# First attention of a two-block transformer: probability tiles turned by diagonal matrices of the shares

## What is computed

```python
def softmax_attend(q, k, v, scale):
    s = jnp.einsum('bqhd,bkhd->bhqk', q, k).astype(jnp.float32) * scale
    p = jax.nn.softmax(s, axis=-1).astype(v.dtype)
    return jnp.einsum('bhqk,bkhd->bqhd', p, v)
...
def window_attend(q, k, v, k_ctx, v_ctx, sink):
    ...
    sink_col = jnp.broadcast_to(sink.reshape(SWA_KV_HEADS, SWA_GROUP, 1, 1).astype(jnp.float32),
                                s_ctx.shape[:-1] + (1,))
```

## Time and profile before

| | us |
|---|---|
| median of 3 runs | 1627.12 (1625.2 to 1627.42) |
| the profiled execution, its own time | 1628.66 |
| its span in the trace | 1626.7 |
| first attention, unit 2's scores to the output projection (109.8 to 237.5 in the span) | 127.7 |
| PE busy in the whole span | 1554.0 |

### The profile page before, as it was taken

One profiled execution on the slowest core, in us unless ns is written; L12 is line 12 of the kernel. 1 busy time (PEld: TensorE's weight loads), 2 busy tenths in 40 slices (PEclk: granted clock), 3 DMA queues, 4 the chain that ended last, 5 costly groups with the idle time before them and its releaser, 6 DMA issues.

```text
span 1626.7 us, 26737 instructions
## 1 busy us (share of the span) xinstructions
PE 1554.0 (96%) x11163; PEld 1203.2 (74%) x11163; DVE 819.1 (50%) x1434; ACT 730.7 (45%) x1122; POOL 0.9 (0%) x5
## 2 busy tenths in 40 slices
PE   8999989999999999999989999999999889999887
PEld 5645667777787778789968999997998778544443
DVE  2536664643333444453486665655686775322123
ACT  3544552633312332362464654535545553554443
POOL 0000000000000000000000000000000000000000
PEclk9999999999999999999999999999999999999999
DMA  9412633344433442433203346453443337899995
GB/s 390 162 39 79 208 109 114 115 156 185 147 122 149 161 157 79 161 110 130 79 1 119 117 150 225 165 165 116 165 139 121 105 102 287 360 420 420 421 420 211
DMA packets 43130, 287.87 MB, mean 177 GB/s; under 512 B 4848, under 2 KB 6000, under 8 KB 12160
## 3 DMA queue, kind: packets, MB, share of 16 engines
q1 hardware_dynamic: 42832, 285.99, 47.1%
q10 hardware_dynamic: 144, 0.06, 0.0%
q0 software_dynamic: 32, 0.07, 0.0%
HBM read 285.05 MB, written 1.05 MB: 176 GB/s over the span
## 4 chain that ended last, share of the span: by engine, by line
PE 80%; DVE 8%; ACT 5%; DMA 5%; issue 2%; SPq 0%; DVEq 0%; ACTq 0%
PE ps L542 16%; PE ps L544 15%; PE ps L543 15%; PE ps L2969 7%; DMA deep<-wts 4%; DVE WL L527 2%; PE ps L593 2%; PE ps L1572 1%; PE ps L1543 1%; PE ps L1474 1%; PE ps L711 1%; PE ps L2830 1%; PE ps L1651 1%; PE ps L1649 1%; PE ps L1650 1%
## 5 line engine op out<-in xcount | busy, mean ns | idle before, releaser
L542 PE MATMUL ps<-HH,WH 128*128 128x256 f32 (+3 forms) x1424 | 467.8, 329 | 14.3 <-DVE WL L527 6.3
L543 PE MATMUL ps<-HL,WH 128*128 128x256 f32 (+3 forms) x1424 | 456.8, 321 | 0.0
L544 PE MATMUL ps<-HH,WL 128*128 128x256 f32 (+3 forms) x1424 | 456.6, 321 | 0.0
L527 DVE TENSOR_TENSOR WL<-ring,WH 128x2048 fp32r<-128x2048 f32 (+2 forms) x134 | 281.6, 2104 | 143.3 <-ACT WH L517 143.3
L542 PEld LDWEIGHTS ps<-HH,WH 128*128 128x128 f32 x1424 | 269.6, 189 | 59.2 <-issue 26.3
L517 ACT ACTIVATE WH<-ring 128x2048 fp32r<-128x2048 f32 (+2 forms) x134 | 236.0, 1763 | 152.1 <-PE ps L544 76.1
L544 PEld LDWEIGHTS ps<-HH,WL 128*128 128x128 f32 x1424 | 269.7, 189 | 20.3
L543 PEld LDWEIGHTS ps<-HL,WH 128*128 128x128 f32 x1424 | 269.9, 190 | 18.2
L2969 PE MATMUL ps<-deep,arena 128*32 128x512 f32 (+1 forms) x872 | 115.3, 593 | 15.5 <-ACT deep L2955 6.8
L542 PE MATMUL ps<-parts,WH 128*128 128x512 f32 (+1 forms) x352 | 120.0, 341 | 0.0
L543 PE MATMUL ps<-parts,WH 128*128 128x512 f32 (+1 forms) x352 | 118.5, 337 | 0.0
(11 more groups left out here) (394 smaller groups left out, 2127.2 us busy)
## 6 DMA issues: line engine op xcount, KB each, us to landing
ring<-wts SPq DMA_DIRECT2D x138, 1024.0 KB, 5.0
deep<-wts SPq DMA_DIRECT2D x92, 1024.0 KB, 18.4
ring<-wts SPq DMA_DIRECT2D x32, 704.0 KB, 4.1
arena<-wts SPq DMA_DIRECT2D x8, 1024.0 KB, 15.4
ring<-wts SPq DMA_DIRECT2D x4, 672.0 KB, 13.7
X<-xin SPq DMA_DIRECT2D x4, 512.0 KB, 16.4
ahead<-wts SPq DMA_DIRECT2D x2, 1024.0 KB, 8.1
deep<-wts SPq DMA_DIRECT2D x4, 512.0 KB, 20.7
```

The source lines that it names most:

```text
L527: e.tensor_tensor(lo, raw(i), hi.bitcast(F32), ALU.subtract).then_inc(*up("low", i))
L542: e.matmul(o, w[0][:, cols], x[0], start=k == 0, stop=False)
L543: e.matmul(o, w[0][:, cols], x[1], start=False, stop=False)
L544: return e.matmul(o, w[1][:, cols], x[0], start=False, stop=k == nk - 1)
```

## The change

Each probability tile is now turned by a real product with a diagonal matrix that holds the shares, instead of by a transpose with the identity; so the turned probabilities are already divided. `share_of` names the diagonal matrices: 64 in all, two for a lat unit and four for a context unit, in three buffers of two matrices each that are used in turn. DVE builds them in `dve_share` (the identity times a share column, a 128x128 TENSOR_SCALAR each), now one step earlier (unit i-1 instead of i-2) and behind the maxima of unit i instead of ahead of them. `pe_values` no longer spreads shares. The copy to `OT` and its multiplication are gone: ACT writes the rounded part straight from PSUM, one step earlier, behind its copy of the turned probabilities; DVE takes the remainder straight from PSUM, where it multiplied before. The bank of an output tile is now freed by that remainder (`o_low`) instead of `o_unit`.

```diff
-        OT = area(256)
+        DG = [area(256)] + [deep[:, a:a + 256] for a in (9 * SLOT + 4096, 9 * SLOT + 16 * NT + 4096)]
...
-                if 0 <= i - 4:
-                    act_values_high(e, i - 4)
...
                 if 0 <= i - 3 < len(UNITS):
-                    act_values(e, i - 3)
+                    act_values_high(e, i - 3)
...
-                if 0 <= i - 2 < len(UNITS):
-                    dve_share(e, i - 2)
                 if i < len(UNITS):
                     dve_scores(e, i)
+                if 0 <= i - 1 < len(UNITS):
+                    dve_share(e, i - 1)
                 if 0 <= i - 4:
-                    dve_values(e, i - 4)
+                    dve_values_low(e, i - 4)
...
-                if 0 <= i - 4:
-                    dve_values_low(e, i - 4)
...
             e.reciprocal(columns(rv, j), c).then_inc(*up("weighed.share", j))
+            e.wait_ge(*at("weighed.share", j))
+            if j >= 2:
+                e.wait_ge(*at("turned_p", j - 2, 1))
+            for s in range(2):
+                for q in range(query_tiles(j)):
+                    t = e.tensor_scalar(share_of(j, s, q), ident, column(rv, j, s, q), None, ALU.mult)
+            t.then_inc(*up("weighed", j))
+        def share_of(j, s, q):
+            n = sum(2 * query_tiles(x) for x in range(j)) + s * query_tiles(j) + q
+            return DG[n // 2 % 3][:, 128 * (n % 2):128 * (n % 2) + 128]
...
                 e.wait_ge(*at("exp", j, s))
+                e.wait_ge(*at("weighed", j))
                 for x in range(4):
-                    c = 128 * x if lat else 256 * (x % 2) + 128 * (x // 2)
-                    t = e.transpose(ps[:, b, 128 * x:128 * x + 128], PA3[j % 3][s][:, c:c + 128], ident)
+                    c, q = (128 * x, 0) if lat else (256 * (x % 2) + 128 * (x // 2), x % 2)
+                    t = e.matmul(ps[:, b, 128 * x:128 * x + 128], PA3[j % 3][s][:, c:c + 128],
+                                 share_of(j, s, q), start=True, stop=True)
...
-            e.wait_ge(*at("weighed.share", j))
-            for q in range(query_tiles(j)):
-                c = 256 + 128 * (qt + q)
-                for s in range(2):
-                    t = e.matmul(ps[64 * s:64 * s + 64, b, c:c + 128], column(rv, j, s, q).to_broadcast([128, 64]), ident,
-                                 start=True, stop=True)
...
-                banks.give(b, "o_unit", ot, lat)
+                banks.give(b, "o_low", ot, lat)
```

More of the change, by code:

```diff
@@ L1571, in pe_values @@
                     v = VM[:, vt, 64 * h:64 * h + 64] if kind == "mla" else VS[:, vt, 64 * s:64 * s + 64]
-                    e.matmul(ps[64 * s:64 * s + 64, b, 128 * qt:128 * qt + nq], v, PTA[:, j % 2, s, nq * kt:nq * kt + nq],
-                             start=kt == 0, stop=kt == nk - 1)
-            e.wait_ge(*at("weighed.share", j))
-            for q in range(query_tiles(j)):
-                c = 256 + 128 * (qt + q)
-                for s in range(2):
-                    t = e.matmul(ps[64 * s:64 * s + 64, b, c:c + 128], column(rv, j, s, q).to_broadcast([128, 64]), ident,
-                                 start=True, stop=True)
+                    t = e.matmul(ps[64 * s:64 * s + 64, b, 128 * qt:128 * qt + nq], v, PTA[:, j % 2, s, nq * kt:nq * kt + nq],
+                                 start=kt == 0, stop=kt == nk - 1)
             t.then_inc(*up("values", j))
             if not lat or qt:
-                banks.give(b, "o_unit", ot, lat)
+                banks.give(b, "o_low", ot, lat)
         def last_of_tile(j):
@@ L1592, in out_key @@
             return out_tile(UNITS[j]), UNITS[j][2]
[L1594 to L1605, removed]
         def act_values_high(e, j):
             if last_of_tile(j):
-                e.wait_ge(*at("o_unit", *out_key(j)))
-                e.activation(out_block(0, j), OT, ACT.Copy).then_inc(*up("o_high", j))
+                e.wait_ge(*at("values", j))
+                e.activation(out_block(0, j), B("o", *out_key(j))[:, 0:256], ACT.Copy).then_inc(*up("o_high", j))
         def dve_values_low(e, j):
@@ L1614, in dve_values_low @@
                 e.wait_ge(*at("o_high", j))
-                e.tensor_tensor(out_block(1, j), OT, out_block(0, j).bitcast(F32),
+                e.tensor_tensor(out_block(1, j), B("o", *out_key(j))[:, 0:256], out_block(0, j).bitcast(F32),
                                 ALU.subtract).then_inc(*up("o_low", *out_key(j)))
```

## The result

The changed kernel takes 1644.35 us (median of 4 runs, 1644.10 to 1645.42) against 1626.27 for the kernel before in the same comparison: ratio 1.0108, 95% interval 1.0095 to 1.012. The prediction was 1643.5 us. (The ratio compares the runs of the two kernels; each kernel's executions differ by 1.3 to 2.2 us among themselves.) The profiled execution took 1644.44 us with a span of 1642.7, 16.0 us more than before.

What follows compares the result with a forecast made beforehand. PE was taken to bound the kernel; +22.1 for the turn, -7.0 spreads, +4.4 bank waits and -3.1 idle time gave +16.4 us, a median of 1643.5 us. Range 1638 to 1650 us (70%), 1635 to 1655 (80%).

Steps and rivals of the forecast that it cites:

- What bounds the kernel: Attention stage: PE is busy 98.3 of 99.8 us before the drain, so what the stage loses is lost.
- The main term: PE's turn: two records per real product, one per transpose; 1.94 us instead of 1.02 a unit, +22.1 us for 24.
- L1766's price: PE's turn: each record of a real product costs 0.115 us, as in the long run of L1766.
- The spreads: PE's share-spreading products L1578 go: 0.22 us at a lat unit, 0.44 at a context unit, 7.0 us gained.
- The bank: PE's turn waits for DVE to free the output tile's bank behind the diagonals: +4.4 us, bounds 1 and 9.
- Idle time taken up: PE's waits in the pipeline's filling (0.7 us) and drain (2.4 us) absorb added work: -3.1 us, bounds 0 and -5.4.
- The sum: Whole kernel: 15.1 + 4.4 - 3.1 = +16.4 us, median 1643.5 us.
- One pass after all: Rival at PE's turn: diagonal products take one record, turn stays 1.02 us; about -2.5 us, 1624.6 us; 7%.
- DVE sets the pace: Rival: costlier diagonals lengthen all 13 bank waits and hold up rotations; +25 us, 1652 us; 8%.
- L1483's price: Rival at PE's turn: each record costs 0.16 us, as for mask product L1483; +31 us, 1658 us; 7%.
- Four times: Rival at PE's turn: real products cost four times the transposes; +66 us, 1693 us; 2%.
- More is hidden: Rival: turn 1.84 us, all 5.4 us of idle time used, bank waits 1 us; +8.3 us, 1635.4 us; 6%.

Runs made afterwards that it cites:

- e1: The kernel before with only the eight transposes of a unit made real products with the identity; 1647.56 us, ratio 1.0123.
- e7: e8 with probability tiles and diagonals in fp32r, the rounded 32-bit type; 1630.13 us, ratio 1.0013.
- e3: The changed kernel with DVE's remainder, which frees the bank, moved ahead of the share and its diagonals; 1640.89 us, ratio 1.0085.
- e8: e3 with share and diagonals moved to the end of DVE's step; 1639.90 us, ratio 1.0088.
- e2: The changed kernel with transposes back in place of the real products, diagonals still built and waited for; 1630.70 us, ratio 1.0023.
- e4: The changed kernel with DVE scaling the probability tile in place instead of building diagonals, transposes kept, remainder ahead of the share; 1628.17 us, ratio 1.0001.
- e9: e5 with ACT's copy of the turned probabilities moved ahead of the modulation's part (output weight rounding, modulation row copy); 1623.69 us, ratio 0.9975.
- e5: e4 with share and scaling moved last in DVE's step; 1623.87 us, ratio 0.9980.
- e6: e4 with two overwritten 128x512 products put ahead of the scores of unit 3 to keep PE at work; 1625.89 us, ratio 0.9995.

## Why the prediction was right, point by point

- **What bounds the kernel.** PE, in this stage without slack, and nothing behind it gives back. The 1388.7 us behind the stage, against 1389.2 before, show it.
- **The main term.** Forecast 1.94 us for a turn, measured 1.98; 24 x 0.96 = 23.0 us instead of 22.1. The step that carried the prediction was counting records against products in the program: two for a product, one for a transpose. e1 shows it alone, and e7 shows what it hangs on. Taking L1766's price and not L1483's was right: a run of sixteen lies near the long run.
- **The spreads.** 7.0 us went from the chain, as forecast.
- **The bank.** Forecast +4.4 us at seven places, measured about 3.5: 0.63, 0.62, 0.95 and 0.46 us at steps 5, 8, 14 and 21, 0.3 us each at 15 and 18, about 0.1 each at 12 and 17. The diagonals were a bit cheaper than taken (two in 0.48 us, the next operation 0.40 behind the first's start). Step 21 was half of what I gave it; PE arrived 0.2 us later than I took, by its wait for ACT's copy, and the rest of the difference is open. e3 gave 3.5 us back.
- **Idle time taken up.** Forecast -3.1 us, measured -1.9: the fill gave 0.32 instead of 0.7, the drain 1.6 instead of 2.4. At step 21 the wait for ACT's copy stayed at 0.50 us (0.58 before), where I had given it 0.3 less. This is the term that was most off, by 1.2 us.
- **The sum.** 23.0 - 7.0 + 3.5 - 1.9 = 17.6 us for a stage that grew by 17.4. My 16.4 hit the whole (16.0 in the profiled span) a little by luck: the main term was 0.9 us too low and the bank 0.9 us too high, and the stage began 0.9 us earlier in this execution, with 0.5 us less behind it. The medians of this comparison differ by 18.1 us; that the forecast time came within 0.9 us of the measured one owes something to the three runs that it started from, whose median was 0.85 us above that of this comparison.
- **The rivals.** One pass after all: refuted by 384 records, though e7 shows that it exists for another type. DVE sets the pace: refuted by e1 and e8. L1483's price: 0.124 us for a record, not 0.16. Four times: refuted; the Trainium skill's factor of four (TensorE: Matmul & The Clock Gate, table of terms) is two in time on the chain here, 1.98 against 1.02 us for products of 128 columns. More is hidden: the turn was 1.98 us and not 1.84, and 1.9 of the 5.4 us of idle time were used.
- **What the forecast did not see** is the clock. It made no difference for the changed kernel, where it stayed full behind the longest waits, 1.01 and 1.48 us, but it took 1.5 to 3.3 us from the profiled executions of e2, e4, e7 and e9.

## What to carry to other kernels

Count the records that one operation of the program leaves in the trace before moving work between kinds of it: in full 32-bit data a 128x128 product with a diagonal or identity leaves two records on PE and takes twice the time of a transpose (0.25 us against 0.13), and eight of them for a unit outweigh a handful of small products that they save. If a scale per row is wanted before a transpose, scale the tile on an engine that has slack, and put that work where nobody waits for it: behind what frees a bank and behind what the next scores need. On a PE that is the bound, each gain moves the wait to the next engine, and a wait on PE can cost more than its length: behind 1.92 and 2.32 us of idle time the clock cost another 1.6 and 3.3 us here.

## What the runs showed of the hardware

- A 128x128 product with 128 columns leaves two records in float32 (16 add 1.98 us) and one in fp32r (8 add 1.04 us), the latter at the price of a float32 transpose (8 add 1.02 us). With 512 columns a float32 product (two records) adds 0.86 us and an fp32r product 0.23 us (before).
- TensorE's clock fell to the 1.2 GHz level behind idle times of 1.92 us (e2), 2.32 us (e4), 1.41 us (e7) and 2.00 us (e9), in one profiled execution each, and stayed at 2.4 GHz behind 1.33 us (before, e5), 1.34 us (e9), 1.71 us (e2, e7), 1.83 us (e4) and 1.87 us (e5). The idle time alone does not order these; what else decides is open.
- With 1.7 us of useless products in such a wait the clock stayed full, and the stage was 3.2 us shorter in the profiled execution (e6 against e4).
- DVE multiplied 128x128 from SBUF by a column in 0.28 us, 0.20 us behind the previous one, 128x256 in 0.35 us and 128x512 in 0.48 us. The Trainium skill (VectorE: DVE Perf Modes, the perf-mode tier table) has this operation at twice the plain rate for 32-bit data in SBUF; the 0.20 us between 0.28 and 0.48 for 384 more columns, 0.52 ns a column, agree with it, against about 1.05 ns a column for operations with two tensors (the product L1605 in the earlier trace rows has 256 columns in 0.41 us, the difference L527 has 2048 in 2.29 us).
